# Partial sums for the norms on VectorE, and the shift's small products moved between later products

## The reference, cut to what matters

```python
# block 1, behind the output projection
x = x + gate1 * mixed
hffn = _rmsnorm(x, norm_ffn_w[l]) * (1.0 + scale2) + shift2
# block 2
h1 = _layer_norm(ALPHA * h + mix, ln1_g[i], ln1_b[i])        # mix: merged @ w_o
ple = sigmoid(h1 @ w_ple_gate[i] + b_ple_gate[i]) * (p[i] @ w_ple[i])
h = _layer_norm(ALPHA * h1 + ffn + ple, ln2_g[i], ln2_b[i])  # ffn: hid @ w_ffn_down
# block 3
h = rms_norm(x, pre_norm1[l]) * (1.0 + sc1) + sh1
proj = h @ w_in[l]
x = x + g1 * rms_norm(y, post_norm1[l])
h = rms_norm(x, pre_norm2[l]) * (1.0 + sc2) + sh2
f = jnp.square(jax.nn.relu(h @ w_ff1[l])) @ w_ff2[l]
x = x + g2 * rms_norm(f, post_norm2[l])
```

## Time and profile before

| what | value |
|---|---|
| time, median of 3 runs | 3095.48 us (3093.12 to 3097.4) |
| the profiled execution's own time | 3097.16 us |
| its span, first to last instruction | 3095.0 us |
| PE busy | 2868.3 us, 93% |
| DVE busy | 1658.7 us, 54% |
| ACT busy | 1018.2 us, 33% |
| mean granted PE clock | 0.97 |

### The profile page before, as it was taken

One profiled execution on the slowest core, in us unless ns is written; L12 is line 12 of the kernel. 1 busy time (PEld: TensorE's weight loads), 2 busy tenths in 40 slices (PEclk: granted clock), 3 DMA queues, 4 the chain that ended last, 5 costly groups with the idle time before them and its releaser, 6 DMA issues.

```text
span 3095.0 us, 37465 instructions
## 1 busy us (share of the span) xinstructions
PE 2868.3 (93%) x15334; PEld 2053.9 (66%) x15334; DVE 1658.7 (54%) x2706; ACT 1018.2 (33%) x1627; POOL 18.8 (1%) x36
## 2 busy tenths in 40 slices
PE   6997888998888899999999999999999978899998
PEld 4875755343434478786576788886867755678887
DVE  6676754332222553439345345556899967453443
ACT  3336233101011333533424222234222266443343
POOL 0000000000000000000000000000000000000000
PEclk8998989999999999999999999999999989999998
DMA  8431004899999622220321345520222200223220
GB/s 292 165 135 55 3 3 163 342 428 427 427 428 428 249 90 74 91 73 28 109 82 48 136 165 209 189 75 28 96 75 92 99 28 28 93 98 109 82 82 28
DMA packets 138180, 453.03 MB, mean 146 GB/s; under 512 B 7216, under 2 KB 10928, under 8 KB 125488
## 3 DMA queue, kind: packets, MB, share of 16 engines
q1 hardware_dynamic: 129968, 434.38, 36.7%
q10 hardware_dynamic: 5760, 8.14, 0.7%
q0 software_dynamic: 2304, 8.39, 0.7%
HBM read 446.70 MB, written 4.19 MB: 146 GB/s over the span
## 4 chain that ended last, share of the span: by engine, by line
PE 72%; DVE 12%; DMA 11%; ACT 3%; issue 2%; SPq 1%; DVEq 0%; ACTq 0%
PE bank L468 16%; PE bank L470 16%; PE bank L469 16%; DMA A<-in_expert_w 9%; PE bank L2027 4%; PE bank L2690 3%; DVE A L3423 2%; PE bank L596 2%; PE bank L1407 1%; DVE ring_parts L464 1%; PE bank L2047 1%; DMA ring<-in_w_ada 1%; PE bank L590 1%; PE bank L3320 1%; DVE small L3659 0%
## 5 line engine op out<-in xcount | busy, mean ns | idle before, releaser
L470 PE MATMUL bank<-A_parts,ring_parts 128*128 128x512 f32 (+1 forms) x1008 | 394.5, 391 | 0.0
L464 DVE TENSOR_TENSOR ring_parts<-ring,A_parts 128x1024 fp32r<-128x1024 f32 x200 | 243.8, 1223 | 258.3 <-ACT A_parts L457 258.1
L457 ACT ACTIVATE A_parts<-ring 128x1024 fp32r<-128x1024 f32 x200 | 209.6, 1053 | 456.6 <-PE bank L470 423.8
L468 PE MATMUL bank<-A_parts 128*128 128x512 f32 x728 | 290.4, 399 | 3.4 <-DVE ring_parts L464 3.2
L469 PE MATMUL bank<-A_parts 128*128 128x512 f32 (+2 forms) x736 | 284.7, 387 | 0.0
L468 PE MATMUL bank<-h_parts,A_parts 128*128 128x512 f32 (+1 forms) x704 | 275.5, 391 | 2.3 <-DVE h_parts L2483 2.3
L469 PE MATMUL bank<-h_parts,A_parts 128*128 128x512 f32 x664 | 259.3, 391 | 0.0
L470 PE MATMUL bank<-h_parts,ring_parts 128*128 128x512 f32 x648 | 253.3, 391 | 0.0
L2027 PE MATMUL bank<-ring,A 128*64 128x512 f32 (+1 forms) x960 | 219.0, 594 | 35.2 <-DMA ring<-in_expert_w 21.5
L470 PEld LDWEIGHTS bank<-A_parts,ring_parts 128*128 128x128 f32 (+1 forms) x1008 | 189.7, 188 | 41.0
L469 PE MATMUL bank<-ring_parts 128*128 128x512 f32 x512 | 200.7, 392 | 0.0
(11 more groups left out here) (664 smaller groups left out, 5227.0 us busy)
## 6 DMA issues: line engine op xcount, KB each, us to landing
ring<-in_expert_w SPq DMA_DIRECT2D x62, 2048.0 KB, 17.4
ring<-in_w_in SPq DMA_DIRECT2D x37, 2048.0 KB, 8.4
A<-in_expert_w SPq DMA_DIRECT2D x33, 2048.0 KB, 21.3
ring<-in_w_ada SPq DMA_DIRECT2D x24, 2048.0 KB, 12.6
ring<-in_w_ff SPq DMA_DIRECT2D x16, 2048.0 KB, 8.0
ring<-in_w_ffn_gate SPq DMA_DIRECT2D x5, 2048.0 KB, 7.6
ring<-in_w_ffn_up SPq DMA_DIRECT2D x5, 2048.0 KB, 7.7
ring<-in_w_o SPq DMA_DIRECT2D x4, 2048.0 KB, 7.9
```

The source lines that it names most:

```text
L457: act.activation(parts(s.shaped(high(s.q % 2))), s.raw(), ACT.Copy).then_inc(sem("split_high"), 1)
L464: eng.tensor_tensor(parts(s.raw()), s.raw(), parts(s.shaped(high(s.q % 2))), ALU.subtract)\
L468: pe.matmul(out, parts(w_high), parts(r_low), start=start, stop=False)
L470: return pe.matmul(out, parts(w_low), parts(r_high), start=False, stop=stop)
```

## The change

In `out` (norm n2), `wo2` (ln1) and `wo3` (post1) DVE adds the first seven tiles, or their squares, into one tile, and PE multiplies that sum once, behind the sixth k step of slice eight, and the last tile once: two constant products in place of eight, each with a wait of its own. In `down2` the first four means become one product of a sum, and in `ff2` the first 16 products of one column become four. The 32 small products of a shift stand in `project_begin` now, four ahead of each k step, in bank 4, and their four DVE operations behind the read of the first two tiles. Where they stood, `in3_early_pe` and `ff1_early_pe` have four products of `keep_busy`; `ffn2_early_pe` has nothing. Slices five and six wait for the small products instead of for the early tiles.

```diff
@@ helpers @@
+        def square_apart(act, n, k, src, acc):
+            if k >= 3:
+                act.wait_ge(sem(f"{n}_added"), k - 2)
+            act.activation(TMP(k % 2) if k else acc, src, ACT.Square).then_inc(sem("norm_squared"), 1)
+
+        def square_add(dve, n, k, acc):
+            dve.wait_ge(*norm_at(n, "squared", k + 1))
+            if k > 1:
+                dve.wait_ge(sem(f"{n}_added"), k - 1)
+            dve.tensor_tensor(acc, acc, TMP(k % 2), ALU.add).then_inc(sem(f"{n}_added"), 1)
+
+        def sum_added(pe, n, acc):
+            pe.wait_ge(sem(f"{n}_added"), KD - 2)
+            pe.matmul(bank[4][:], sq("mean"), acc, start=True, stop=False).then_inc(sem("norm_summed"), KD - 1)
+
+        def sum_last(pe, n):
+            pe.wait_ge(*norm_at(n, "squared", KD))
+            pe.matmul(bank[4][:], sq("mean"), TMP((KD - 1) % 2), start=False, stop=True).then_inc(sem("norm_summed"), 1)
+
+        def shift_products(pe, n, step, slices, high, shift):
+            s = slices[step // 4]
+            if step == 0:
+                pe.wait_ge(sem(f"{n}_split"), 1)
+            for k in range(2 * (step % 4), 2 * (step % 4) + 2):
+                pe.matmul(bank[4][:, 2 * (step // 4):2 * (step // 4) + 2], parts(s.shaped(high(s.q % 2))[:, k, :]),
+                          parts(shift[:, k, :]), start=(k == 0), stop=False)
+                mm = pe.matmul(bank[4][:, 2 * (step // 4):2 * (step // 4) + 2], parts(s.raw()[:, k, :]),
+                               parts(shift[:, k, :]), start=False, stop=(k == KD - 1))
+            if step % 4 == 3:
+                mm.then_inc(sem(f"{n}_mapped"), 1)
@@ out_pe, add_gated (out3_pe, out3_dve alike, with "post1") @@
-                          behind=lambda k: norm_sum(pe, "n2", k, TMP))
-            norm_sum(pe, "n2", KD - 1, TMP)
+                          behind=lambda k: sum_added(pe, "n2", n2_squares) if k == KD - 2 else None)
+            sum_last(pe, "n2")
...
+                if j >= 2:
+                    square_add(dve, "n2", j - 1, n2_squares)
@@ hg_pe, hg_dve @@
+        def wo_sum_pe(pe):
+            pe.wait_ge(sem("wo_added"), KD - 2)
+            pe.matmul(bank[5][:], sq("mean"), wo_sum, start=True, stop=False)
...
-                          first=lambda k: pe.wait_ge(sem("merged_split"), k + 1), behind=lambda k: wo_mean(pe, k))
+                          first=lambda k: pe.wait_ge(sem("merged_split"), k + 1), behind=lambda k: wo_sum_pe(pe) if k == KD - 2 else None)
...
+                if j >= 2:
+                    dve.wait_ge(sem("tile_read"), tile)
+                    if j > 2:
+                        dve.wait_ge(sem("wo_added"), j - 2)
+                    dve.tensor_tensor(wo_sum, wo_sum if j > 2 else X(0), X(j - 1), ALU.add).then_inc(sem("wo_added"), 1)
@@ ffn2 (in3 and ff1 alike, with shift1 and shift3) @@
+        def shift0_step(pe, k):
+            if k == 0:
+                pe.wait_ge(*norm_at("ln1", "std", 1))
+            shift_products(pe, "shift0", k, ffn_early, ffn_high, shift0)
+
         def ffn2_early_pe(pe):
-            pe.wait_ge(sem("shift0_split"), 1)
-            for s in ffn_next:
-                bank_free(pe, s.g.first_tile + s.m)
-            for i, s in enumerate(ffn_early):
-                w_high = s.shaped(ffn_high(s.q % 2))
-                pe.wait_ge(sem("split_low"), s.q + 1)
-                for k in range(KD):
-                    pe.matmul(shift0_bank(i)[:, 0:2], parts(w_high[:, k, :]), parts(shift0[:, k, :]), start=(k == 0),
-                              stop=False)
-                    mm = pe.matmul(shift0_bank(i)[:, 0:2], parts(s.raw()[:, k, :]), parts(shift0[:, k, :]), start=False,
-                                   stop=(k == KD - 1))
-                mm.then_inc(sem("shift0_mapped"), 1)
+            pe.wait_ge(sem("split_low"), ffn_early[1].q + 1)
...
-            project_begin(pe, ffn_next, ffn_next_high, Hn, x_low, lambda k: norm_at("ln1", "out", k + 1),
+            project_begin(pe, ffn_next, ffn_next_high, Hn, x_low, lambda k: shift0_step(pe, k) or norm_at("ln1", "out", k + 1),
...
-            means(range(4))
+            pe.wait_ge(sem("down_added"), 3)
+            pe.matmul(bank[5][:], sq("mean"), down_sum, start=True, stop=False)
@@ in3_early_pe, ff1_early_pe: in place of the 32 small products @@
+            keep_busy(pe, 4, 7)
+            pe.wait_ge(sem("split_low"), in3_early[1].q + 1)
@@ u1_lows (u0_lows, u3_lows alike); the two operations stand behind the read of tile j now @@
-                for i in range(2):
-                    dve.wait_ge(sem("shift1_mapped"), i + 1)
-                    step(dve.tensor_copy(shift1_out[:, i:i + 1], shift1_bank(i)[:, 0:1]))
-                    dve.tensor_tensor(shift1_out[:, i:i + 1], shift1_out[:, i:i + 1], shift1_bank(i)[:, 1:2], ALU.add)\
-                        .then_inc(sem("shift1_kept"), 1)
@@ out3_pe @@
-            for k in range(4):
-                pe.wait_ge(*norm_at("post2", "squared", k + 1))
-                f_sum_pe(pe, k, ff2_square(k))
+            pe.wait_ge(sem("f_added"), 3)
+            f_sum_pe(pe, 3, ff2_square(0))
@@ out3_dve @@
+                    for k in range(1, 4):
+                        if k > 1:
+                            dve.wait_ge(sem("f_added"), k - 1)
+                        dve.tensor_tensor(ff2_square(0), ff2_square(0), ff2_square(k), ALU.add)\
+                            .then_inc(sem("f_added"), 1)
```

More of the change, by code:

```diff
@@ L9 @@
+from collections import namedtuple
 from contextlib import ExitStack
@@ L397, in project_deep @@
                 k_at = 0 if last else k_at + g.kt
+        Freed = namedtuple("Freed", "free")
         class Slice:
@@ L3274, in build, with shift1_step @@
         L["ff1"][3].also = ("tile_ready", L["wo3"][-1].first_tile + 4)
+        def shift1_step(pe, k):
+            if k == 0:
+                pe.wait_ge(*norm_at("pre1", "std", 1))
+            shift_products(pe, "shift1", k, in3_early, in3_high, shift1)
         def in3_early_pe(pe):
-            pe.wait_ge(sem("shift1_split"), 1)
-            for s in in3_next:
-                bank_free(pe, s.g.first_tile + s.m)
-            for i, s in enumerate(in3_early):
-                w_high = s.shaped(in3_high(s.q % 2))
-                pe.wait_ge(sem("split_low"), s.q + 1)
-                for k in range(KD):
-                    pe.matmul(shift1_bank(i)[:, 0:2], parts(w_high[:, k, :]), parts(shift1[:, k, :]), start=(k == 0),
-                              stop=False)
-                    mm = pe.matmul(shift1_bank(i)[:, 0:2], parts(s.raw()[:, k, :]), parts(shift1[:, k, :]), start=False,
-                                   stop=(k == KD - 1))
-                mm.then_inc(sem("shift1_mapped"), 1)
+            keep_busy(pe, 4, 7)
+            pe.wait_ge(sem("split_low"), in3_early[1].q + 1)
             for s in in3_early:
@@ L3309, in in3_pe @@
         def in3_pe(pe):
-            project_begin(pe, in3_next, in3_next_high, in3_x_high, Hn, lambda k: norm_at("pre1", "out", k + 1),
+            project_begin(pe, in3_next, in3_next_high, in3_x_high, Hn, lambda k: shift1_step(pe, k) or norm_at("pre1", "out", k + 1),
                           lambda k: pe.wait_ge(*seen("h3_in_split", k + 1)))
@@ L3745, in out3_pe @@
                           first=lambda k: pe.wait_ge(sem("merged3_split"), 5 + k // 4),
-                          behind=lambda k: norm_sum(pe, "post1", k, TMP))
-            norm_sum(pe, "post1", KD - 1, TMP)
+                          behind=lambda k: sum_added(pe, "post1", post1_squares) if k == KD - 2 else None)
+            sum_last(pe, "post1")
             ff1_early_pe(pe)
-            project_begin(pe, ff1_next, ff1_next_high, lambda k: W(32 + k), Hn, lambda k: x_turn_pe(pe, k) or norm_at("pre2", "out", k + 1),
+            project_begin(pe, ff1_next, ff1_next_high, lambda k: W(32 + k), Hn, lambda k: shift3_step(pe, k) or norm_at("pre2", "out", k + 1),
                           lambda k: pe.wait_ge(*seen("h3_split", k + 1)))
@@ L3795, in x_turn_act, with shift3_step @@
             act.activation(W(28 + g) if g < TT else X(g - TT), bank[5 + g % 3][:], ACT.Copy).then_inc(sem("x_turn_kept"), 1)
-        def ff1_early_pe(pe):
-            pe.wait_ge(sem("shift3_split"), 1)
-            for s in ff1_next:
-                bank_free(pe, s.g.first_tile + s.m)
-            for i, s in enumerate(ff1_early):
-                w_high = s.shaped(ff1_high(s.q % 2))
-                pe.wait_ge(sem("split_low"), s.q + 1)
-                for k in range(KD):
-                    pe.matmul(shift3_bank(i)[:, 0:2], parts(w_high[:, k, :]), parts(shift3[:, k, :]), start=(k == 0),
-                              stop=False)
-                    mm = pe.matmul(shift3_bank(i)[:, 0:2], parts(s.raw()[:, k, :]), parts(shift3[:, k, :]), start=False,
-                                   stop=(k == KD - 1))
-                mm.then_inc(sem("shift3_mapped"), 1)
+        def shift3_step(pe, k):
+            if k == 0:
```

(15 more changed lines are left out.)

52 lines of the change are left out of this document (36 added, 16 removed).

## The result

The changed kernel took 3067.09 us, the median of 4 runs (3062.18 to 3068.68), against 3094.91 for the kernel before (3093.12 to 3097.4, 4 runs): the ratio is 0.99, with an interval of 0.9887 to 0.9912, so 27 to 35 us less by the ratio and 27.8 by the medians. The profiled execution took 3068.68, 28.5 less than the profiled one of before. The forecast was 3070.

A forecast was written before the change was run, and what follows sets the result against it. It took PE's own list to bound the kernel wherever PE waits for nobody (72% of the chain). Terms summed to -27.4 against the profiled 3097.2, giving 3069.8, taken as 3070; forecast 3067 to 3074 (chance 0.50), range 3064 to 3080.

The forecast's parts named there:

- the stall at the place named: In `wo2`, the sum product behind slice eight's sixth step waits 0.7 for DVE's last addition; bounds none or 1.5.
- `ln1`: First u product starts at 1664.9, at full clock, sums 1.78 apart: term -4.9, low bound -2.6 if the clock falls.
- `pre1`'s start: Ahead of `pre1`, `keep_busy` keeps the clock up, 1.1, and moved DVE operations give 0.5: -1.6.
- `pre2`'s: At `pre2`'s start, `keep_busy` avoids seven products at 0.43 instead of 0.23: -1.4.
- PE the bound in `pre2`: Four small products make a step 1.35 against ACT's 1.33, so PE never catches up: +1.8.
- The steps behind `ln1`'s norm: In `ln1`, four small products a step, 0.46 at full clock, fit in PE's 0.59 of idle time: nothing.
- the half-clock sum that I made for `pre1`: In `pre1`, a half-clock step takes 1.72 against 1.33, 0.39 late for four or five steps: +1.8, bounds 0 and 3.
- the prediction's own signs of being wrong: A sum product waiting over 2 us, a slice still above 6, or the clock falling at new places.
- `ff2`'s 5.9: Four one-column products for 16 give -3.4; with no clock fall behind them, -5.9 in all; low bound -2.4.
- Rival 1: Clock falls anyway in `ln1`'s idle time, `ff2` and all `pre1` steps: +2.3, +3.5, +1.5, so 3077; chance 0.26, part or full.
- Rival 2: Small products keep the clock up, so `pre1`'s 1.8 is nothing: 3068; chance 0.15 together with the no-stall rival.
- Rival 3: No stall and nothing late in `wo2`, `wo3` and `pre2`: 3067; chance 0.15 together with the rival on small products.
- Rivals 4 and 5: No change, saved PE time returns as addition waits, chance 0.03; slower, ACT held by the additions, 3122, chance 0.03.

The follow-up runs named there:

- `add_first`: The changed kernel with DVE's last addition in `wo2`, at tile eight, moved ahead of that turn's low parts; 3069.1 us, ratio 0.9908 to the kernel before.
- `no_busy`: The changed kernel without the four constant products ahead of the u products in `pre1` and in `pre2`; 3073.21 us, ratio 0.9918 to the kernel before.
- `shift_only`: The kernel before with only the moved small products and the constant products ahead of `pre1` and `pre2`, sums as before; 3090.3 us, ratio 0.997.
- `four_sums`: The changed kernel with the four sums of `ff2` as before, 16 one-column products; 3073.58 us, ratio 0.9926 to the kernel before.
- `best`: The changed kernel with `wo2`'s addition first, a wide product per `ln1` and `pre1` step, half of `pre2`'s small products ahead; 3066.3 us, ratio 0.9892.
- `wide`: The changed kernel with each step's four small products replaced by two of 512 columns, the shift's own sum not computed; 3066.26 us, ratio 0.9892.

## Why the prediction came out as it did

**Right by its own steps.** The constant products cost 0.86 each: `down2` gave 2.54 for three. `wo2` gave 4.70 against 4.5 forecast, with the stall at the place named (0.51 idle, 0.76 as a price; forecast 0.7), and `add_first` showed that the pile of low parts makes it. In `wo3` the same product waits 0.21, where I took 0.3. `ln1` gave 4.83 against 4.9: the first u product came 2.75 behind the mean product and the sums followed 1.78 apart. `pre1`'s start, 1.51 against 1.6, and `pre2`'s, 1.26 against 1.4, rest on the constant products ahead, as `no_busy` shows. Four small products and a transpose group make PE the bound in `pre2`: +1.54 against +1.8, 1.31 a step where I had worked out 1.35 (2707.83 to 2709.14, line 3842).

**Off in a term.** The steps behind `ln1`'s norm were booked at nothing, since PE idles there. They cost 1.04, as the clock fell (0.58 in the window from 1680). The step that failed is "In `ln1` PE idles 0.59 at each step: nothing", which holds at full clock only; the half-clock sum that I made for `pre1` (1.72 against 1.33) was due here too. It also took the steps of before to run at full clock to their end, and they did not (windows of the kernel before):

```profile
1696.00:1698.00 2.00, 1.65 (x4) 1.36 (x5) 1.87 (x4) 1.98 (x3) 0.00 (x0) 0.63 0.00 0
1698.00:1700.00 2.00, 2.00 (x6) 1.52 (x6) 1.42 (x2) 1.99 (x4) 0.00 (x0) 0.52 0.00 0
```

In three of six profiles with these four small products a step the clock stayed up (`shift_only`, `add_first`, `four_sums`), and the part gained 1.69 to 1.70. In `add_first` the steps up to 1696.4 of before are as far ahead as the last sums (15.1 and 15.0), so there the small products cost nothing; 1.6 is gained from 1696.4 to 1700.3, where before had its half clock. In the changed kernel's two profiles the clock fell sooner, for longer, and the part lost 1.0; in `no_busy` it was down for about half as long (0.53 and 0.61 from 1682 to 1686) and the part gained 0.30. So the term is anything from -1.7 to +1, by the clock alone. The fall in the changed kernel is also one of the prediction's own signs of being wrong, a fall at a new place: 1680 in the changed kernel is 1695 in before, where the clock was 1.00. In `pre1` the clock fell in all six, and that cost 0.8 to 1.6 against 1.8 forecast.

In `pre1`'s start the working has a slip: 1.1 for the clock and 0.5 for the DVE operations make the 1.6, and the 0.4 by which four constant products are shorter than the small ones (3.4 and 3.8) is left out. Measured were 1.13 for the clock, by `no_busy`, and 0.38 for all the rest.

Of `ff2`'s 5.9, 4.3 belong to the change; 1.6 was where the clock happened to fall in the one profile that the sum was made from. In the total the changed parts give -26.6 (the table's column, with 0.4 of routing in its row `out`), 0.8 short of the sum of 27.4, and its unchanged ones -1.7 of their own; the last 0.2 of the 28.5 lies outside these parts. That the total came so close is partly luck: code that nobody touched gave more than the changed parts fell short.

**The rivals.** Rival 1, the clock falls in `ln1`'s idle time, did not come in the changed kernel's two profiles but did in `shift_only` and `best`; its price was 1.4 and 1.2 there (2.3 forecast). The argument against it, that 0.59 of idle in each 1.33 had not made the clock fall, was weak: 3 us on, in the same steps, the windows of before shown above have 0.63 and 0.52. Rival 2 is out by `pre1`, where the clock fell in all six profiles with small products alone, and by `wide`. The Trainium skill (TensorE: Matmul & The Clock Gate, Part 1) has the gate go by how busy PE has been. By PE's busy time in the profile these traces do not bear it out: the windows busy for 1.74 and 1.75 us had clocks of 0.58 and 1.00. Rival 3's missing stall was made by hand in `add_first`. Rivals 4 and 5 are out: a slice takes 5.44, and only one product a projection waits. What stays open is why an idle time of the same length brings the clock down in one run and not in another; no run here tells that.

## What to carry to other kernels

Work on TensorE's own list, where it waits for nobody, is worth its length, and a sum over tiles can go to an idle vector engine if its last addition doesn't stand behind a pile of other work. The two-column products here took time without holding the clock up; put such products where their step has slack even at half clock, or put a wide product beside them. A gain read from one profile at half clock is partly luck: split each such term into what holds at full clock and what hangs on the fall, and look at unchanged stages to see how much the clock moves by itself.

## What the hardware showed

Two small products start 0.11 us apart at full clock and 0.21 at half (1678.34 to 1678.45, 1681.48 to 1681.69), in the changed kernel as in the earlier trace rows. The Trainium skill (TensorE: Matmul & The Clock Gate, LDWEIGHTS) gives a weight load as its columns over 1.2, which is 107 ns for 128, and names no clock. The first pair agrees, the second does not.

More work made a stretch shorter: with a product that nobody uses in each step (`fill`), `pre1`'s steps took 2.7 us less than in the changed kernel.
